# The starting addresses of TensorE's moving operands in SBUF, in a fused two-block kernel

## The chip, the cores and the metric

The kernel runs on one core of one Trainium2 chip. The metric is the device time of one execution in microseconds (us), as the median of several executions. Engines are named as in the profile: PE is TensorE's matmul side, PEld its weight loads, DVE VectorE, ACT ScalarE, POOL GpSimd, SP the queue that issues the DMAs.

## What is computed

Two transformer-like blocks run over one sequence of 256 tokens with 2048 features, all in float32. Cut to the matrix products that matter here:

```python
mod = silu(c) @ w_ada + b_ada                      # six modulation vectors
h = rmsnorm(x) * (1 + sc) + sh                     # 256 x 2048
q, k, v, g_ret, u, gate_r, gate_s = split(h @ w_in)
y_ret = (silu(g_ret) * norm(retention(q, k, v))) @ w_ret_out
y_s5  = glu(gelu(s5_ssm(u)) @ w_s5_glu)
x = x + gt * rmsnorm((sigmoid(gate_r)*y_ret + sigmoid(gate_s)*y_s5) @ w_out)
x = x + gt2 * rmsnorm((silu(a) * b) @ w_ffn_out)   # a, b = split(h2 @ w_ffn_in)
# second block: projections of h for attention, gated linear attention, convolution
mixed = g0 * (o_att @ w_br_attn) + g1 * (o_gla @ w_br_gla) + g2 * (y_conv @ w_br_conv)
x = x + mixed @ w_out_2
x = x + (silu(h4 @ w_gate) * (h4 @ w_up)) @ w_down
out = rmsnorm(x)
```

The weight matrices are large (703 MB are read), the 256 tokens few, so nearly all the time goes into products of a 128x128 piece of weights with 256 tokens.

## The kernel before

Features stand on the 128 partitions, the 256 tokens (T) in the free dimension. Every activation that is multiplied with large weights is kept as two float32r halves that together carry the float32 value: `h_split[P, 16, 512]` holds, for each of 16 tiles of features, 256 words of the high half and then 256 words of the low half. The same layout have `ffn1_split` and `ffn2_split` (the profile calls both ffn_split), `ret_split`, `merged_split`, `y_ssm_split`, `o_att_split`, `o_gla_split`, `y_conv_split` and `mixed_split`. These are the large moving operands.

Weights come through a ring of four slots. SP loads 1 MB into `ring_raw`, ACT writes the high half `ring_hi` (line 1017), DVE the low half `ring_lo` (line 1477), and PE uses them for one product. A product goes over 16 tiles of 128 features, and `products` (lines 632 to 639) is its inner step. It has two forms, which the text calls the pair and the triple:

- The pair, lines 638 and 639: the high weights times both halves of the moving operand (512 columns), then the low weights times the high half (256 columns), into two halves of one PSUM bank which DVE adds up later (line 1492). The stages from the first feed-forward on use it.
- The triple, lines 635, 636 and 637, three matmuls of 256 columns that add up in the same place. The stages `u`, `heads`, `ret`, `glu` and `out1` of the first block use it.

Both stream 768 moving columns per tile of 128 features. Each matmul has its own weight load of 128 columns. Everything else that PE does is small: sums of squares (lines 687 to 694), the retention, attention and gated-linear-attention products, the S5 steps (lines 705 and 715), the products of the value heads (line 734), and `gate_down` (lines 894 and 895), which multiplies `h_split` with only 16 columns of weights, `wa_hi` and `wa_lo`.

The order is written out by hand for each engine and tied by semaphores. Nothing in it depends on an address. SBUF is laid out by nested `with` blocks: `sb(stack, name, shape)` takes the next free place on the stack, rounded up to 32 bytes, and a block's places are free again when it closes. So a tensor's address is the sum of what was opened before it.

Of the kernel before, what the change touches and what calls it, by code (L numbers as in the profile page):

```python
# [29 lines left out]
P = 128  # L30
# [5 lines left out]
HEADS = 8  # L36
# [166 lines left out]
def program(nc, dram, out):  # L203
    stored, ph = schedule(), stages()
    with ExitStack() as ctx:
        def sb(stack, name, shape, dt=F32):
            return stack.enter_context(nc.sbuf_tensor(name, shape, dt))
# [26 lines left out]
        tile = [sb(ctx, f"tile{i}", [P, T]) for i in range(2)]  # L234
        eps = sb(ctx, "eps", [P, 4])
        root_of_one = sb(ctx, "root_of_one", [P, 1])

        with ExitStack() as shared:
            y2 = sb(shared, "y2", [P, KT, T])
# [6 lines left out]
        with ExitStack() as block1:  # L246
            c_act = sb(block1, "c_act", [P, D])
            with ExitStack() as mixer:
                log_g = sb(mixer, "log_g_sb", [P, HEADS])
                wv = [[], []]  # L250
                with ExitStack() as shared:
                    wv[0] = [sb(shared, f"wv_a{n}", [P, 4, 4, P]) for n in range(4)]
                with ExitStack() as shared:
                    v_heads = sb(shared, "v_heads", [P, HEADS, 4, T])
                with ExitStack() as shared:
                    ret = sb(shared, "ret_split", [P, HEADS, 2, 2 * T], F32R)
                with ExitStack() as shared:
                    first_gates = sb(shared, "first_gates", [P, 4, 2 * T])
                merged = sb(mixer, "merged_split", [P, KT, 2 * T], F32R)
                with ExitStack() as shared:  # L260
                    sb(shared, "y_ssm_first", [P, HALF // 2, 2 * T])
                    aside_y = sb(shared, "aside_y", [P, D])
                with ExitStack() as shared:
                    wv[1] += [sb(shared, f"wv_b{n}", [P, 4, 4, P]) for n in range(2)]
                y_ssm = sb(mixer, "y_ssm_split", [P, HALF, 2 * T], F32R)
                with ExitStack() as shared:
                    aside_z = sb(shared, "aside_z", [P, D])
                sb(mixer, "before_lag", [P, T])
                lag = sb(mixer, "lag_sb", [P, T])
                rope = sb(mixer, "rope_sb", [P, 2, T])  # L270
                with ExitStack() as shared:
                    aside_u = sb(shared, "aside_u", [P, D])
                with ExitStack() as shared:
                    wv[1].append(sb(shared, "wv_b2", [P, 4, 4, P]))
                u = sb(mixer, "u", [P, HALF, T])
                s5_a = sb(mixer, "s5_a_sb", [P, 3, S5_TILES])
                s5_d = sb(mixer, "s5_d_sb", [P, HALF])
                s5_turn = sb(mixer, "s5_turn", [P, 2, S5_TILES, RAMP])
                s5_r = sb(mixer, "s5_r", [P, S5_TILES])
                s5_f = sb(mixer, "s5_f", [P, S5_TILES, 2, 2])  # L280
                with ExitStack() as shared:
                    aside_s = sb(shared, "aside_s", [P, D])
                s5_b = [sb(mixer, f"s5_b_sb{i}", [P, 2, P]) for i in range(2)]
                s5_c = [sb(mixer, f"s5_c_sb{i}", [P, 2, P]) for i in range(2)]
                s5_prod = sb(mixer, "s5_prod", [P, 2, 2, 32])
                s5_x = [sb(mixer, f"s5_x{i}", [P, 2, T]) for i in range(2)]
                s5_y = sb(mixer, "s5_y", [P, T])
                s5_g = sb(mixer, "s5_g", [P, T])
                with ExitStack() as shared:
                    wv[1].append(sb(shared, "wv_b3", [P, 4, 4, P]))  # L290
                with ExitStack() as retention:
                    aside_r = sb(retention, "aside_r", [P, D])
                    qk_rot = sb(retention, "qk_rot", [P, 2, T])
                    g_act = sb(retention, "g_act", [P, 2, T])
                    scores = sb(retention, "scores", [P, 384])
                    o_t = sb(retention, "o_t", [P, 2, T])
                    gn_stats = sb(retention, "gn_stats", [P, 2, 6])
                    gn_mean = sb(retention, "gn_mean", [P, 2, 2])
                    gn_spare = sb(retention, "gn_spare", [P, 2])
                with ExitStack() as after:  # L300
                    m_ret = sb(after, "m_ret", [P, KT, T])
                    gate = sb(after, "gate", [P, T])
                    val_a = sb(after, "val_a", [P, T])
                    val_b = sb(after, "val_b", [P, T])
                with ExitStack() as before:
                    c_tanh_half = sb(before, "c_tanh_half", [P, D])
                    s5_t = sb(before, "s5_t", [P, 12, S5_TILES])
                    s5_step = sb(before, "s5_step", [P, RAMP])
                    s5_round = sb(before, "s5_round", [P, 2, S5_TILES, RAMP])
                with ExitStack() as after:  # L310
                    y1 = sb(after, "y1", [P, KT, T])
            with ExitStack() as ffn:
                f1 = sb(ffn, "ffn1_split", [P, FF, 2 * T], F32R)
                f1_a = [sb(ffn, f"ffn1_a{i}", [P, T]) for i in range(2)]
                f1_b = [sb(ffn, f"ffn1_b{i}", [P, T]) for i in range(2)]
                f1_t = [sb(ffn, f"ffn1_t{i}", [P, T]) for i in range(2)]


        with ExitStack() as block2:
            with ExitStack() as mixer:  # L320
# [27 lines left out]
                    a_end = sb(early, "a_end", [P, GLA_HEADS, T])  # L348
                t0 = sb(mixer, "merge0", [P, KT, T])
                conv_w = sb(mixer, "conv_w_sb", [P, HALF, 3])  # L350
                with ExitStack() as early:
                    gq = sb(early, "gq", [P, T])
                    gk = sb(early, "gk", [P, T])
                    gv_t = sb(early, "gv_t", [P, 2, T])
                    gr_t = sb(early, "gr_t", [P, 2, T])
                    gr_act = sb(early, "gr_act", [P, 2, T])
                    q_in = [sb(early, f"q_in{i}", [P, T]) for i in range(2)]
                    k_in = sb(early, "k_in", [P, T])
                    k_dec = sb(early, "k_dec", [P, T])
                    gv_n = sb(early, "gv_n", [P, 2, T])  # L360
                    k_dec_n = sb(early, "k_dec_n", [P, 3, P])
                    intra = sb(early, "intra", [P, 2, P])
                    state = [sb(early, f"state{i}", [P, T]) for i in range(3)]
                    go = sb(early, "go", [P, 2, T])
                    go_sq = sb(early, "go_sq", [P, 2, T])
                    go_std = sb(early, "go_std", [P, T])
                    go_rstd = sb(early, "go_rstd", [P, T])
                    att_q = [sb(early, f"att_q{i}", [P, T]) for i in range(2)]
                    att_k = [sb(early, f"att_k{i}", [P, T]) for i in range(2)]
                    att_v = [sb(early, f"att_v{i}", [P, T]) for i in range(2)]  # L370
# [2025 lines left out]
```

## Time and profile before

| | |
|---|---|
| median of three runs | 3384.47 us (3382.92 to 3384.51) |
| the profiled execution, whole | 3381.64 us |
| its span, first to last instruction | 3379.9 us |
| PE busy, share of the span | 98% |
| PEld / DVE / ACT / POOL busy | 87% / 69% / 43% / 13% |
| mean granted clock of PE | 0.992 of 2.4 GHz |
| DMA | 706 MB, mean 209 GB/s |

The trace gives each instruction's start and duration. A matmul's duration is longer than the step from its start to the next one's, because matmuls are pipelined. So what a matmul costs in a long stream is read from starts: the first start, a later one, and the number of matmuls between them. That step is what the text calls cadence.

### The profile page before, as it was taken

The page shows a single profiled execution, that of the slowest core. Times are in us where ns is not written, and L with a number is a line of the kernel's source. Part 1 is how long each engine was busy: PE and PEld are TensorE (multiplying, and loading weights), DVE is VectorE, ACT ScalarE, POOL GpSimd, SP SyncE. Part 2 cuts the span into 40 slices and gives each one's busy share as a digit, 9 for nine tenths or more (in the row PEclk, how much of TensorE's full clock was granted, in tenths as well). Part 3 has the DMA queues.
Part 4 walks back from the last instruction along what each step waited for, and adds up shares of the span by engine and source line. Part 5 has one row for each costly group of instructions (what it writes and reads, how often), then busy time and mean ns, then how long its engine had stood idle before and what let it go on. Part 6 is the DMA issues. An engine that isn't in the chain of part 4 may idle for free.

```text
span 3379.9 us, 51972 instructions
## 1 busy us (share of the span) xinstructions
PE 3307.3 (98%) x20368; PEld 2937.2 (87%) x20368; DVE 2324.5 (69%) x2503; ACT 1452.4 (43%) x1464; POOL 435.2 (13%) x309
## 2 busy tenths in 40 slices
PE   6999999999899999999899999999999999999998
PEld 3599999999788888888788888888888888888887
DVE  6789979877766666666666667566767766666554
ACT  2256664444443444433454443444344444344332
POOL 1047668500100000000000000000003000000000
PEclk9999999999999999999999999999999999999999
DMA  9885456678545555577534444555555555555554
GB/s 378 349 328 180 180 202 237 251 292 311 198 175 188 192 191 186 195 268 254 198 137 169 167 162 178 193 183 186 192 186 196 188 188 186 189 192 186 185 191 149
DMA packets 119746, 706.34 MB, mean 209 GB/s; under 512 B 13776, under 2 KB 28752, under 8 KB 41312
## 3 DMA queue, kind: packets, MB, share of 16 engines
q1 hardware_dynamic: 109280, 695.96, 56.2%
q10 hardware_dynamic: 10368, 9.02, 0.8%
q8 instruction: 68, 1.11, 0.1%
q14 instruction: 30, 0.25, 0.0%
HBM read 702.83 MB, written 2.10 MB: 209 GB/s over the span
## 4 chain that ended last, share of the span: by engine, by line
PE 90%; DVE 5%; ACT 1%; DMA 1%; SPq 1%; issue 1%; DVEq 0%; ACTq 0%
PE acc L638 45%; PE acc L639 24%; PE acc L635 6%; PE acc L636 6%; PE acc L637 6%; DVE ring_raw L1499 1%; DVE ring_lo L1477 1%; DMA ring_raw<-w_ada 1%; SPq L542 1%; PE p_y L705 1%; PE p_norm L687 1%; PE p_z L715 1%; ACT ring_hi L1017 0%; DMA ring_raw<-w_out 0%; DVE rstd L1524 0%
## 5 line engine op out<-in xcount | busy, mean ns | idle before, releaser
L638 PE MATMUL acc<-h_split,ring_hi 128*128 128x512 f32 x4736 | 1655.9, 392 | 9.5 <-DVE h_split L1539 4.5
L1477 DVE TENSOR_TENSOR ring_lo<-ring_raw,ring_hi 128x2048 fp32r<-128x2048 f32 (+2 forms) x560 | 1265.1, 2260 | 550.2 <-ACT ring_hi L1017 549.1
L639 PE MATMUL acc<-h_split,ring_lo 128*128 128x256 f32 x4736 | 1337.6, 282 | 0.0
L1017 ACT ACTIVATE ring_hi<-ring_raw 128x2048 fp32r<-128x2048 f32 (+2 forms) x560 | 1040.0, 1862 | 458.6 <-DMA ring_raw<-w_down 150.4
L638 PEld LDWEIGHTS acc<-h_split,ring_hi 128*128 128x128 f32 x4736 | 891.9, 188 | 197.6 <-issue 10.0
L639 PEld LDWEIGHTS acc<-h_split,ring_lo 128*128 128x128 f32 x4736 | 897.9, 190 | 0.4
L638 PE MATMUL acc<-ffn_split,ring_hi 128*128 128x512 f32 x1408 | 488.2, 390 | 0.0
L2146 POOL TENSOR_TENSOR sq_sum<-sq_sum,tile 128x256 f32<-128x256 f32 x60 | 79.6, 1326 | 2561.6 <-ACT tile L1043 2561.6
L639 PE MATMUL acc<-ffn_split,ring_lo 128*128 128x256 f32 x1408 | 397.1, 282 | 0.0
L635 PE MATMUL acc<-h_split,ring_hi 128*128 128x256 f32 x1152 | 329.2, 286 | 0.3 <-ACT val_a L1030 0.2
L637 PE MATMUL acc<-h_split,ring_lo 128*128 128x256 f32 x1152 | 321.6, 279 | 0.0
L636 PE MATMUL acc<-h_split,ring_hi 128*128 128x256 f32 x1152 | 321.6, 279 | 0.0
L638 PEld LDWEIGHTS acc<-ffn_split,ring_hi 128*128 128x128 f32 x1408 | 264.4, 188 | 55.4
L639 PEld LDWEIGHTS acc<-ffn_split,ring_lo 128*128 128x128 f32 x1408 | 266.1, 189 | 0.0
L635 PEld LDWEIGHTS acc<-h_split,ring_hi 128*128 128x128 f32 x1152 | 216.6, 188 | 1.8 <-issue 0.6
L636 PEld LDWEIGHTS acc<-h_split,ring_hi 128*128 128x128 f32 x1152 | 216.6, 188 | 1.1 <-issue 0.2
L637 PEld LDWEIGHTS acc<-h_split,ring_lo 128*128 128x128 f32 x1152 | 216.6, 188 | 0.0
L1310 ACT ACTIVATE ffn_split<-ffn_a 128x256 f32 (+1 forms) x88 | 36.8, 418 | 361.5 <-DVE ffn_a L1903 361.5
L1492 DVE TENSOR_REDUCE ffn_b<-acc 128x256 f32<-128x512 f32 x88 | 60.8, 691 | 143.2 <-PE acc L639 143.2
L1043 ACT ACTIVATE tile<-x_res 128x256 f32 (+1 forms) x80 | 33.1, 417 | 152.1 <-DVE x_res L2127 85.2
L1308 ACT ACTIVATE ffn_t<-ffn_a 128x256 f32<-128x256 f32 x88 | 36.7, 417 | 129.3 <-DVE ffn_a L1899 119.2
L2204 POOL TENSOR_TENSOR s_x<-s_w,s_tab 128x512 f32<-128x512 f32 x32 | 86.6, 2707 | 29.9 <-DVE s_w L1688 29.8
(381 smaller groups left out, 3936.5 us busy)
## 6 DMA issues: line engine op xcount, KB each, us to landing
ring_raw<-w_ff SPq DMA_DIRECT2D x88, 1024.0 KB, 4.8
ring_raw<-w_down SPq DMA_DIRECT2D x64, 1024.0 KB, 4.8
ring_raw<-w_ffb SPq DMA_DIRECT2D x56, 1024.0 KB, 4.8
ring_raw<-w_mix SPq DMA_DIRECT2D x48, 1024.0 KB, 4.8
ring_raw<-w_ada SPq DMA_DIRECT2D x32, 1024.0 KB, 11.9
ring_raw<-w_heads SPq DMA_DIRECT2D x32, 1024.0 KB, 4.8
ring_raw<-w_ret SPq DMA_DIRECT2D x32, 1024.0 KB, 5.2
ring_raw<-w_glu SPq DMA_DIRECT2D x32, 1024.0 KB, 4.9
```

The costliest lines, as they stand in the source:

```text
L635: mm(dst[:, 0:T], hi[s][:, t, :], moving[:, k, 0:T], start=start, stop=False)
L636: mm(dst[:, 0:T], hi[s][:, t, :], moving[:, k, T:], start=False, stop=False)
L637: return mm(dst[:, 0:T], lo[s][:, t, :], moving[:, k, 0:T], start=False, stop=stop)
L638: mm(dst[:], hi[s][:, t, :], moving[:, k, :], start=start, stop=False, skip_group_check=True)
L639: return mm(dst[:, T:], lo[s][:, t, :], moving[:, k, 0:T], start=False, stop=stop, skip_group_check=True)
L1017: run(hi[s][:, 0:n, :], raw[s][:, 0:n, :], COPY).then_inc(hi_done, 1)
L1308: run(t[i % 2][:], a[i % 2][:], ACT.Tanh, scale=0.5).then_inc(f_tanh, 1)
L1310: run(dst[:, 4 * g + (first + i), 0:T], a[i % 2][:], COPY, scale=0.5).then_inc(f_hi, 1)
L1477: tt(lo[s][:, 0:n, :], raw[s][:, 0:n, :], hi[s][:, 0:n, :], SUB).then_inc(lo_done, 1)
L1492: v.tensor_reduce(dst, acc[o % 2][:].rearrange("p (c t) -> p t c", c=2), AX_X, ADD).then_inc(sum_done, 1)
L2146: tt(sq_sum[:], sq_sum[:], tile[b][:], ALU.add).then_inc(sq_used, 1)
L2204: tt(xs[:], w[:], sin, ALU.mult)
```

## The change

Three lines are added and one is moved. `log_g` (8 words, 32 bytes) is taken before `h_split` and not in the mixer of block 1, and two unused tensors of 32 bytes are put in. No instruction is added, taken away or moved: on every engine the instructions stand in the same order with the same waits, and only addresses differ.

```diff
@@ -234,6 +234,7 @@
         eps = sb(ctx, "eps", [P, 4])
         root_of_one = sb(ctx, "root_of_one", [P, 1])
+        log_g = sb(ctx, "log_g_sb", [P, HEADS])
...
@@ -246,7 +247,6 @@
             with ExitStack() as mixer:
-                log_g = sb(mixer, "log_g_sb", [P, HEADS])
                 wv = [[], []]
...
@@ -275,6 +275,7 @@
                 s5_d = sb(mixer, "s5_d_sb", [P, HALF])
+                sb(mixer, "s5_space", [P, 8])
                 s5_turn = sb(mixer, "s5_turn", [P, 2, S5_TILES, RAMP])
...
@@ -348,6 +349,7 @@
                 conv_w = sb(mixer, "conv_w_sb", [P, HALF, 3])
+                sb(mixer, "conv_space", [P, 8])
                 with ExitStack() as early:
```

The addresses of the built programs, as the remainder by 128. Each operand's tiles are 2048 bytes apart and its low half begins 1024 bytes behind the high one, so every matmul on it starts at the same remainder.

| tensor | form | before | after |
|---|---|---|---|
| `h_split` | pairs and triples | 32 | 64 |
| `ffn1_split`, `ffn2_split` | pairs | 32 | 64 |
| `o_att_split`, `o_gla_split`, `y_conv_split` | pairs | 32 | 64 |
| `mixed_split` | pairs | 0 | 64 |
| `ret_split`, `merged_split`, `y_ssm_split` | triples | 64 | 64 |
| `wv_a`, `u` (float32, moving) | small products | 64 | 64 |
| `s5_x` (float32, moving) | S5 steps | 96 | 0 |
| `ring_raw`, `ring_hi`, `ring_lo` (weights) | all | 0 | 0 |
| `wa_hi`, `wa_lo` (weights of `gate_down`) | 16 columns | 32 | 64 |
| `x_res`, `tile`, `rstd` | | 0, 96, 96 | the same |

The smaller tensors that lie above these on the stack shift by 32 or 64 bytes with them.

## Rows read from the trace of the kernel before

**Rows 1.** The page: busy time; the chain that ended last, by engine and line.
```profile
PE 3307.3 (98%) x20368; PEld 2937.2 (87%) x20368; DVE 2324.5 (69%) x2503; ACT 1452.4 (43%) x1464; POOL 435.2 (13%) x309
PE 90%; DVE 5%; ACT 1%; DMA 1%; SPq 1%; issue 1%; DVEq 0%; ACTq 0%
PE acc L638 45%; PE acc L639 24%; PE acc L635 6%; PE acc L636 6%; PE acc L637 6%; DVE ring_raw L1499 1%; DVE ring_lo L1477 1%; DMA ring_raw<-w_ada 1%; SPq L542 1%; PE p_y L705 1%; PE p_norm L687 1%; PE p_z L715 1%; ACT ring_hi L1017 0%; DMA
```

**Rows 2.** Groups of PE by shape: count | busy us, mean ns | idle us.
```profile
L638 PE MATMUL acc<-h_split,ring_hi 128*128 128x512 f32 x4736 | 1655.9, 392 | 9.5 <-DVE h_split L1539 4.5 <-DVE h_split L1537 4.4 <-DVE ffn_a L1492 0.4
...
L638 PE MATMUL acc<-ffn_split,ring_hi 128*128 128x512 f32 x1408 | 488.2, 390 | 0.0
...
L636 PE MATMUL acc<-h_split,ring_hi 128*128 128x256 f32 x1152 | 321.6, 279 | 0.0
...
L636 PE MATMUL acc<-ret_split,ring_hi 128*128 128x256 f32 x256 | 71.5, 279 | 0.0
...
L636 PE MATMUL acc<-merged_split,ring_hi 128*128 128x256 f32 x256 | 70.7, 276 | 0.0
```

**Rows 3.** Timeline of PE, pairs on h_split: start us, us, engine, line.
```profile
999.84 0.39 PE L638 MATMUL acc<-h_split,ring_hi 128*128 128x512 f32 x1
...
1032.77 0.39 PE L638 MATMUL acc<-h_split,ring_hi 128*128 128x512 f32 x1
```

**Rows 4.** Timeline of PE, pairs on mixed_split, the first product's 16.
```profile
2542.53 0.40 PE L638 MATMUL acc<-mixed_split,ring_hi 128*128 128x512 f32 x1
...
2548.14 0.39 PE L638 MATMUL acc<-mixed_split,ring_hi 128*128 128x512 f32 x1
```

**Rows 5.** Timeline of PE, triples in the glu stage: h_split, y_ssm_split, h_split again.
```profile
703.80 0.28 PE L635 MATMUL acc<-h_split,ring_hi 128*128 128x256 f32 x1
...
709.41 0.28 PE L635 MATMUL acc<-y_ssm_split,ring_hi 128*128 128x256 f32 x1
...
714.85 0.28 PE L635 MATMUL acc<-h_split,ring_hi 128*128 128x256 f32 x1
```

**Rows 6.** Timeline of PE, one product of triples on ret_split, and what follows it.
```profile
464.76 0.28 PE L635 MATMUL acc<-ret_split,ring_hi 128*128 128x256 f32 x1
...
470.41 0.38 PE L705 MATMUL p_y<-s_x,s_c_sb 128*128 128x256 f32 x1
```

**Rows 7.** Timeline of PE, the slowest product of triples on h_split.
```profile
692.60 0.28 PE L635 MATMUL acc<-h_split,ring_hi 128*128 128x256 f32 x1
...
698.35 0.28 PE L635 MATMUL acc<-y_ssm_split,ring_hi 128*128 128x256 f32 x1
```

**Rows 8.** Timeline of PE, gate_down: pairs on h_split with 16 columns of weights.
```profile
1699.47 0.39 PE L894 MATMUL p_score<-h_split,wa_hi 128*16 128x512 f32 x1
...
1704.69 0.39 PE L894 MATMUL p_score<-h_split,wa_hi 128*16 128x512 f32 x1
```

**Rows 9.** Timeline of PE: float32 products of 512 columns; then pairs at half clock.
```profile
79.66 1.02 PE L734 MATMUL p_o<-wv_b,normed 128*128 128x512 f32 x2
...
81.37 1.02 PE L734 MATMUL p_z<-wv_b,normed 128*128 128x512 f32 x2
...
1731.24 0.41 PE L639 MATMUL acc<-h_split,ring_lo 128*128 128x256 f32 x1
...
1733.80 0.41 PE L639 MATMUL acc<-h_split,ring_lo 128*128 128x256 f32 x1
```

**Rows 10.** Waits of PE; stretches, busy of PE PEld DVE ACT POOL, PEclk, DMA.
```profile
PE acc L638 <- DVE h_split L1539: 4.5, 1, 4.5
...
1731.30:1733.70 2.40, 2.40 (x9) 2.11 (x8) 1.92 (x2) 2.40 (x7) 0.00 (x0) 0.50 0.00 0
...
2300.00:2500.00 200.00, 200.00 (x1156) 177.31 (x1155) 139.70 (x154) 79.69 (x72) 0.00 (x0) 1.00 0.52 189
```

**Rows 11.** Two groups of ACT on the page, of the same form.
```profile
L1310 ACT ACTIVATE ffn_split<-ffn_a 128x256 f32 (+1 forms) x88 | 36.8, 418 | 361.5 <-DVE ffn_a L1903 361.5
...
L1043 ACT ACTIVATE tile<-x_res 128x256 f32 (+1 forms) x80 | 33.1, 417 | 152.1 <-DVE x_res L2127 85.2
```

## The prediction

> **What bounds the kernel now.** First the page's busy times and the chain of waits: PE is busy for 98% of the span and carries 90% of the chain that ended last, 87% of it in the five lines of `products` [rows 1]. So the question is what one of these matmuls costs, and next how many there are of each kind: the groups by shape [rows 2] give 4736 pairs on h_split and 1408 on ffn_split. o_att, o_gla and y_conv have 16 products of 8 pairs each, 384, which makes 6528 pairs at remainder 32. mixed_split has 16 products of 16 pairs, 256, at remainder 0. h_split has also 1152 triples at 32 [rows 2], which is 72 products of 48 matmuls.
>
> The durations in the groups don't give the cost, since matmuls overlap. The timeline does. From 999.84 to 1032.77 lie 95 pairs on h_split: 32.93 us / 95 = 346.6 ns each [rows 3]. The product on mixed_split, at remainder 0, has 16 pairs in 5.61 us, 350.6 ns each [rows 4]. Both ran at full clock, with the same ring of weights, 768 columns, no wait inside. The address is the one difference I can name, so a pair feels it, by 4 ns between 0 and 32. What a pair costs at 64 no row shows: all pairs of this kernel stand at 0 or 32.
>
> The triples do show 64. Side by side in the glu stage, 48 matmuls on h_split (remainder 32) take 5.61 us, 116.9 ns each, and the 48 behind them on y_ssm_split (64) take 5.44 us, 113.3 ns [rows 5]. All 16 products on merged_split and the last 11 of 16 on y_ssm_split look like that; the mean duration goes with it, 276 ns in the middle matmul on merged_split [rows 2]. But 64 has a second, slower cadence: a product on ret_split takes 5.65 us, 117.7 ns each [rows 6]. 15 of 16 products on ret_split, with a mean of 279 [rows 2], and the first 5 on y_ssm_split have it. merged_split has the same address as ret_split, so the address alone doesn't decide which cadence a product falls into. Remainder 32 has a slow cadence too, 5.75 us or 119.8 ns [rows 7], but in one product of 72, and in no stretch of pairs.
>
> Is the loss in the weight loads? `gate_down` loads 16 columns of weights in place of 128 and still takes 5.22 us for 15 pairs, 348.0 ns [rows 8]. So shorter loads don't help, and what is lost is on the side of the moving operand. Is it a fixed price of each matmul? Float32 products of 512 columns pass twice: from the first of two on p_o to the first of two on p_z, with two on p_norm between, four start in 1.71 us, 427.5 ns each for 1024 column steps [rows 9], hardly above 1024 / 2.4. At half clock four pairs take 2.56 us, 640 ns each [rows 9], which is 768 / 1.2 exactly; the granted clock there is 0.50 [rows 10]. The overhead is there only when float32r columns are asked for at 2.4 per ns: a pair takes 346.6 where 768 / 2.4 is 320.0. That fits a reader of SBUF that can't quite keep up and for which the start within some unit matters. The Trainium skill ("TensorE: Matmul & The Clock Gate", Back-to-back issue gap) gives N / 2.4 + 2.5 ns for a warm matmul, whatever the address. By that a pair would take 325.0 before and after and the change would do nothing. The measured 346.6 and 350.6 decide against it.
>
> **The change part by part.** No instruction moves, so every term is a count times a change of cadence, on the engine that sets the end.
>
> Pairs from 32 to 64, 6528 of them. The bounds: nothing below 320.0 (a gain of 26.6 ns) and, above, three matmuls at 117.7, 353.1 (a loss of 6.5). Between them two readings of the good cadence. A triple at 64 takes 3 x 113.3 = 340.0 for the same 768 columns. Or a pair keeps its relation to a triple, which at 32 is 346.6 / 350.7: then it takes 340.0 x 346.6 / 350.7 = 336.0. I take 340.0, since it is the row itself, and keep 336.0 for the range: 6528 x 6.6 = 43.1 us saved.
>
> Pairs on mixed_split from 0 to 64, 256: 256 x (350.6 - 340.0) = 2.7 us saved.
>
> Triples on h_split from 32 to 64, 72 products. The 61 that stand before 690 us in the trace share their stages with ret_split and the early y_ssm_split, whose 64 was slow in 20 of 21. I let them follow: 61 x 48 x (117.7 - 116.8) = 2.6 us lost. The 11 later ones gain: 11 x (5.61 - 5.44) = 1.9 us saved. Together 0.7 us lost. If all were at 113.3, they would save 61 x 48 x 3.5 + 1.9 = 12.1 us, and ret_split and y_ssm_split another 20 x 48 x 4.4 = 4.2 us.
>
> What stays at nothing: ret_split, merged_split and y_ssm_split keep their remainder. s5_x goes from 96 to 0, but its float32 products pass at half rate like those of [rows 9], and the longest of them are a few hundred matmuls. In the few pairs at half clock the address can't show, since their 640 ns hold no overhead [rows 9]. The shifted tensors of ACT and DVE: ACT takes 418 ns to write ffn_split at 32 and 417 to write tile at 96 [rows 11], so I give them no cost. Both engines have slack anyway: in a typical stretch of 200 us DVE is busy 139.7 and ACT 79.7, at 189 GB/s [rows 10].
>
> Is a shorter product covered by the others? A product of 16 pairs would go from 5.55 to 5.44 us. DVE needs 139.7 / 200 x 5.55 = 3.9 of it. PE waits for no low half of the ring in the steady stages: the largest wait of a product is a stage's opening, 4.5 us [rows 10]. DMA would go from 189 to 193 GB/s. So the gain arrives whole. Those waits stay.
>
> The sum: -43.1 - 2.7 + 0.7 = -45.1 us against the profiled execution's 3381.6, which is 3336.5. The median lies 2.8 above that execution, so 3339.
>
> **The rivals.**
>
> Deeper: pairs at 336.0 and all triples at 113.3: 6528 x 10.6 + 256 x 14.6 + 16.3 = 89.2 us saved, 3295. For it speaks that a pair is one matmul less than a triple and was 4.1 ns cheaper at 32. Halfway to it lies 3317.
>
> The slow cadence (the other side): pairs at 64 lock into the one that ret_split shows. Scaled as above, 353.1 x 346.6 / 350.7 = 349.0, a loss of 2.4 ns a pair. 6528 x 2.4 = 15.7 us lost, 0.4 won on mixed_split, 72 x 48 x 0.9 = 3.1 lost on h_split, and 5.9 (28 x 48 x 4.4) if the fast products at 64 fell too: 24.3 us, 3409. It decides above 347.6 ns for a pair: from there the kernel is slower by over 0.2%. For it: 20 of 48 products at 64 are slow, and I know no cause. Against: they all lie in the first 690 us, in and just behind the S5 stages. From there on all 27 products at 64 are fast, and the stages of pairs all lie later. And pairs at 32 hold one cadence through every wait.
>
> Nothing happens: 32 and 64 are alike for a pair, and the gap between the triples comes from something else in the stage. Then only the triples move, from 0.7 lost to 16.3 saved: 3385, or 3367. The mechanism would be a unit of 16 or 32 bytes, of which 0, 32 and 64 are all multiples. The Trainium skill ("SBUF — State Buffer", in the part on the DMA port swizzle) states lines of 16 bytes, and by it alone the change leaves the time at 3384. Against it: mixed_split at 0 and h_split at 32 differ in the same form and the same ring [rows 3, 4].
>
> That the change doesn't do what it says I leave out: the addresses of the built program show all of the large operands at 64.
>
> **How the numbers follow.** Chances: the forecast 0.42, the deeper case 0.15, pairs unchanged with triples gaining 0.08, nothing 0.12, the slow cadence 0.20, something slower still 0.03. A measurement of this kernel can tell about 0.2% from no change, 6.8 us. Faster: 0.42 + 0.15 + 0.08 = 0.65. Same: 0.12, and 0.01 of the slow case. Slower: 0.22. The range goes from 3300, which cuts off the deep end, to 3412, which takes in the slow case. The likeliest case alone has 3315 to 3350.
>
> **What would show it.** In the trace after, the timeline of a stretch like [rows 3]: 95 pairs should take 32.3 us, not 32.9; the product on mixed_split 5.44 us, not 5.61; h_split in glu 5.44, not 5.61. A window like that from 2300 us should hold about 1177 matmuls in 200 us, not 1156 [rows 10]. If the pairs show 349 or more, the step that failed is the carrying over of a triple's cadence to a pair. If pairs are faster and the span isn't, PE has new waits on the low halves of the ring, from DVE.

## The result, and the profile after

The changed kernel takes 3431.26 us (median of four, 3429.51 to 3434.0) against 3384.07 for the kernel before on the same occasion: a ratio of 1.0141, 95% interval 1.0123 to 1.0158. It is slower by 47 us, where 45 us less were forecast. The span of the profiled execution grew from 3379.9 to 3432.2, by 52.3 us. That is 5 us more than the medians differ: the profile before is of one of that kernel's quicker executions (3381.64 us), the profile after of the slowest of four (3434.0). Every cadence below is read from one execution of its kernel.

The page after, the rows that answer to [rows 1]; line numbers are two higher than before.

```profile
PE 3358.9 (98%) x20368; PEld 2949.1 (86%) x20368; DVE 2327.5 (68%) x2503; ACT 1452.1 (42%) x1464; POOL 433.0 (13%) x309
PE 90%; DVE 5%; DMA 2%; ACT 1%; SPq 1%; issue 1%; DVEq 0%; ACTq 0%
```

PE's busy time grew by 51.6 us, that of its loads by 11.9, and no other engine's by more than 3.0. The bound is the same, and it is the matmuls that cost more. The wait of PE that [rows 10] shows and one stretch, in the changed kernel:

```profile
PE acc L640 <- DVE h_split L1541: 4.5, 1, 4.5
...
2300.00:2500.00 200.00, 200.00 (x1134) 174.15 (x1133) 136.59 (x152) 79.36 (x71) 0.00 (x0) 1.00 0.50 184
```

1134 matmuls in 200 us, where 1156 stood before and 1177 were forecast. In this stretch DVE and ACT are less busy and the clock is full. PE's waits for other engines add up to 60.4 us before and 61.1 after, so they explain under 1 us. Single ones did move: a wait of a small product on p_norm, before and then after, grew by 3.8 us, and two others shrank by 3.2 together.

```profile
PE p_norm L765 <- DVE o_t L1730: 0.4, 1, 0.4
```

```profile
PE p_norm L767 <- DVE o_t L1732: 4.2, 1, 4.2
```

The timelines of PE in the changed kernel, for [rows 3, 4, 5]: pairs on h_split, pairs on mixed_split, triples on h_split in the glu stage.

```profile
999.75 0.39 PE L640 MATMUL acc<-h_split,ring_hi 128*128 128x512 f32 x1
...
1032.96 0.40 PE L640 MATMUL acc<-h_split,ring_hi 128*128 128x512 f32 x1
...
2589.79 0.40 PE L640 MATMUL acc<-mixed_split,ring_hi 128*128 128x512 f32 x1
...
2623.71 0.40 PE L640 MATMUL acc<-mixed_split,ring_hi 128*128 128x512 f32 x1
...
709.12 0.28 PE L637 MATMUL acc<-h_split,ring_hi 128*128 128x256 f32 x1
...
714.77 0.28 PE L637 MATMUL acc<-y_ssm_split,ring_hi 128*128 128x256 f32 x1
```

94 pairs on h_split in 33.21 us are 353.3 ns each (346.6 before). 96 pairs on mixed_split in 33.92 us are 353.3 (350.6). 48 matmuls in 5.65 us are 117.7 (116.9). Both traces hold the same 20368 matmuls in the same order, so the steps can be compared one by one. Over the whole trace the steps of the 6528 pairs grew by 42.4 us, about 6.5 ns a pair, and those of the 256 on mixed_split by 0.6 us. Alone in a stream a pair grew by 6.7 ns; between small matmuls it grew less (h_split at 352.4 ns there in the changed kernel).

Another part came from operands whose address didn't change. Triples on merged_split (their third matmuls), before and then after:

```profile
839.98 0.28 PE L637 MATMUL acc<-merged_split,ring_lo 128*128 128x256 f32 x1
...
845.76 0.28 PE L637 MATMUL acc<-merged_split,ring_lo 128*128 128x256 f32 x1
```

```profile
839.75 0.28 PE L639 MATMUL acc<-merged_split,ring_lo 128*128 128x256 f32 x1
...
845.75 0.28 PE L639 MATMUL acc<-merged_split,ring_lo 128*128 128x256 f32 x1
```

Both fences hold 17 triples: 5.78 us, 340.0 ns each, and 6.00 us, 353 ns. All of merged_split and y_ssm_split is at 353.3 ns now, so 27 products of 16 triples lost 13.3 ns each: 5.7 us. The triples on h_split took 2.4 us more. Together that is 51.1 of the 52.3 us; the rest lies in the small products and in the waits. Neither merged_split nor the ring moved by a byte between these two kernels. So the 5.7 us need not be the doing of the change. The spans of the two profiles differ by 5 us more than the medians, which is about as much, and there is no second trace of either kernel to show whether these triples have the same cadence in each execution.

### The profile page after: what moved, and what is told of

Same layout as the page of the kernel before. It is cut to its first block, busy times and chain, and to the rows that moved or that the text cites. A ratio compares the mean times of both kernels' runs of the same rounds, so it can differ in the third digit from the quotient of the medians.

```text
span 3432.2 us, 51972 instructions
## 1 busy us (share of the span) xinstructions
PE 3358.9 (98%) x20368; PEld 2949.1 (86%) x20368; DVE 2327.5 (68%) x2503; ACT 1452.1 (42%) x1464; POOL 433.0 (13%) x309
## 4 chain that ended last, share of the span: by engine, by line
PE 90%; DVE 5%; DMA 2%; ACT 1%; SPq 1%; issue 1%; DVEq 0%; ACTq 0%
PE acc L640 46%; PE acc L641 24%; PE acc L637 5%; PE acc L638 5%; PE acc L639 5%; DVE ring_raw L1501 1%; DVE ring_lo L1479 1%; DMA ring_raw<-w_ada 1%; SPq L544 1%; PE p_y L707 1%; PE p_z L717 1%; PE p_norm L689 1%; ACT ring_hi L1019 0%; DMA ring_raw<-w_u 0%; DVE rstd L1526 0%
## 5 line engine op out<-in xcount | busy, mean ns | idle before, releaser
L640 PE MATMUL acc<-h_split,ring_hi 128*128 128x512 f32 x4736 | 1688.3, 398 | 9.4 <-DVE h_split L1541 4.5
L640 PE MATMUL acc<-ffn_split,ring_hi 128*128 128x512 f32 x1408 | 497.6, 396 | 0.0
L640 PE MATMUL acc<-mixed_split,ring_hi 128*128 128x512 f32 x256 | 90.5, 397 | 0.0
```

Source lines behind the costliest of these rows:

```text
L640: mm(dst[:], hi[s][:, t, :], moving[:, k, :], start=start, stop=False, skip_group_check=True)
```

## The experiments

The question is what the address of the moving operand is counted from. Two facts of the timeline give the candidates: in long streams of these two kernels pairs have one cadence at one address, and the load of the next weights starts with the matmul (2 to 4 ns behind its start in the changed kernel). The changed kernel at 1000 us:

```profile
1000.10 0.40 PE L640 MATMUL acc<-h_split,ring_hi 128*128 128x512 f32 x1
1000.10 0.19 PEld L641 LDWEIGHTS acc<-h_split,ring_lo 128*128 128x128 f32 x1
1000.33 0.28 PE L641 MATMUL acc<-h_split,ring_lo 128*128 128x256 f32 x1
1000.34 0.19 PEld L640 LDWEIGHTS acc<-h_split,ring_hi 128*128 128x128 f32 x1
```

So two streams are read from SBUF at once, the moving operand and the next weights. Theory A: the moving operand's own remainder decides. Theory B: the distance between the two streams decides. Theory C: the way a stage is entered decides. All kernels below are the changed kernel with other spacers, unless said otherwise. In the kernel before and in the change every ring tensor has the remainder 128 by 256. "Distance" is the moving operand's address less the weights', from the second group on modulo 256.

**All operands at 32, 96, 0, and the weights at 32.** One more spacer behind `log_g`, of 96, 32 and 64 bytes. The fourth has 32 bytes ahead of the ring and 96 behind `log_g`.

```diff
+        sb(ctx, "ring_space", [P, 8])          # r32_m64 only
         raw, hi, lo = [], [], []
...
         log_g = sb(ctx, "log_g_sb", [P, HEADS])
+        sb(ctx, "moving_space", [P, 24])       # m32, r32_m64; 8 in m96, 16 in m0
```

> All large moving operands at remainder 32, the ring of weights at 0 as before. Theory A (the moving operand's own remainder by 128 sets the cadence) and theory B (the distance between moving operand and weights sets it) agree here: pairs 346.7 ns, those on mixed_split too (before 351.0), triples about 350, time within 3 us of 3384. Theory C (the cadence is a matter of how a stage is entered, not of addresses): pairs keep any of 346.7 or 353.3, so a stage or two may differ.

Measured: ratio to before 1.0015 (1.0005 to 1.0024). All pairs at 346.7 ns, those on mixed_split too. The triples are slower than before, at 352 to 354 ns.

> All large moving operands at remainder 96, weights at 0. Theory B, if distances of 32 to either side count alike: pairs 346.7 ns as at 32, about 3385 us. Theory A says nothing on 96 ahead of the run; if the cadence goes with the number of 64-byte units touched, 96 is like 32 (346.7), if it grows with the remainder it is above 353.3, over 3431 us.

Measured: 1.0109 (1.0092 to 1.0126). Pairs 350.0 ns, but 353.0 on mixed_split; triples 360.0, near the slow cadence of [rows 7], in every product. Neither guess of the expectation, 346.7 or above 353.3, was right.

> All large moving operands at remainder 0, weights at 0. Both A and B carry over what mixed_split showed before: pairs 351.0 ns, so 6528 x 4.3 = 28 us over before, about 3412 us. Theory C: pairs at 346.7 or 353.3.

Measured: 1.0105 (1.0088 to 1.0122). Pairs 351.1 ns as expected, 353.3 on mixed_split, triples 356. The time is 3419.83 us, 8 more than expected; the slower triples were not in the estimate.

> Moving operands at remainder 64 as in the change, but the ring of weights at 32 (and x_res, ident, ones and the other tensors behind it 32 further on). The distance between the two is 32, as before the change. Theory A: pairs 353.3 ns, about 3431 us. Theory B: pairs 346.7 ns, about 3384 us.

Measured: 1.0009 (0.9999 to 1.0018). Pairs 346.7 ns, with the moving operands at remainder 64. That is against theory A and for B. The same stretch in m96, m0 and r32_m64, with 1145, 1141 and 1156 matmuls:

```profile
1000.00:1200.00 200.00, 200.00 (x1145) 174.26 (x1144) 125.75 (x126) 81.86 (x71) 0.00 (x0) 1.00 0.52 187
```

```profile
1000.00:1200.00 200.00, 200.00 (x1141) 175.27 (x1141) 127.13 (x125) 80.41 (x71) 0.00 (x0) 1.00 0.52 185
```

```profile
1000.00:1200.00 200.00, 200.00 (x1156) 176.03 (x1155) 127.51 (x127) 82.45 (x72) 0.00 (x0) 1.00 0.53 190
```

mixed_split was the odd one out: it had the same remainder by 128 as the others and another cadence. By 256 its address differs from theirs by 128. Ordered by distance modulo 256, the pairs of all these runs fall into one table.

| distance from both kinds of weights | ns a pair | seen on |
|---|---|---|
| 0 | 353.3 | mixed_split in m0 |
| 32 | 346.7 | kernel before; mixed_split in m32 and r32_m64 |
| 64 | 353.3 | change |
| 96 | 350.0 | m96 |
| 128 | 351.1 | m0; mixed_split in the kernel before |
| 160 | 346.7 | m32, r32_m64 |
| 192 | 353.2 | mixed_split in the change |
| 224 | 353.0 | mixed_split in m96 |

**Low and high weights apart, first try.** Spacers within each slot of the ring, so that the high weights lie 32 bytes off the low ones by 128.

```diff
             lo.append(sb(ctx, f"ring_lo{s}", [P, KT, P], F32R))
+            sb(ctx, f"hi_space{s}", [P, 8])    # hi32_lo0; 24 in hi0_lo32
             hi.append(sb(ctx, f"ring_hi{s}", [P, KT, P], F32R))
+            sb(ctx, f"lo_space{s}", [P, 24])   # hi32_lo0; 8 in hi0_lo32
```

hi0_lo32 has besides 32 bytes ahead of the ring and 96 behind `log_g`.

> The changed kernel, moving operands at 64, low weights at 0, high weights at 32. So the distance from the weights to the moving operand is 64 for the low and 32 for the high weights. PE starts the load of the next weights 2 to 3 ns after a matmul's start. Theory B1 (what counts is the distance to the weights that are loaded during a matmul): the 512-column step runs beside a load of low weights at distance 64 and stays near 233.6 ns, the 256-column step runs beside a load of high weights at distance 32 and falls to about 118; pair about 352, time about 3423 us. Theory B2 (what counts are a matmul's own weights): 512-column step about 229, 256-column step 119.7, pair about 348.5, 3400 us.

Measured: 1.0076 (1.0059 to 1.0093), pairs 350.0 ns in both feed-forward blocks and in the long streams on h_split beside them, but from 347.3 (h_split) to 353.4 (o_gla) in the stages between.

> The mirror of the kernel with high weights at 32: low weights at 32, high weights at 0, moving operands at 64. B1: 512-column step about 229, 256-column step 119.7, pair about 348.5, 3400 us. B2: pair about 352, 3423 us. If the two mixtures come out alike, the load and the stream couple over the whole pair and neither theory splits it rightly.

Measured: 1.0056 (1.004 to 1.0073), pairs 349.8 ns, from 348.8 to 350.8 by operand. In the feed-forward blocks the two mixtures came out alike. But by 256 the slots lie 128 apart in turn here, so each kernel mixes two distances. They decide nothing between B1 and B2.

**Distances of 16 and 48.** The ring's tensors begin 16 or 48 bytes into their space, by a view. By 256 the high weights then lie 128 bytes from the low ones.

```diff
...
-            lo.append(sb(ctx, f"ring_lo{s}", [P, KT, P], F32R))
+            lo.append(sb(ctx, f"ring_lo{s}", [P, KT * P + 4], F32R)[:, 4:].rearrange("p (k c) -> p k c", k=KT))
+            sb(ctx, f"lo_space{s}", [P, 24])
...
```

> Moving operands at 64, all ring weights at 16: distance 48. If the cadence runs smoothly between the distances measured (32: 346.7, 64: 353.3), the pair is near 350.0 and the time near 3408 us. If only the unit of 32 bytes counts, which a distance falls into, it is one of the two, 346.7 or 353.3.

Measured: 1.0035 (1.0024 to 1.0046). Distance 48 from the low and 176 from the high weights, and two cadences at the same addresses: 351.1 ns in the first feed-forward block, 346.7 in the second. The changeover lies between 1742 and 2059 us, in the stages where each product is followed by small matmuls. mixed_split, at 176 from the low and 48 from the high weights, has 344.5, the fastest pair seen. The run had 1141 matmuls in the first stretch and 1156 in the second:

```profile
1000.00:1200.00 200.00, 200.00 (x1141) 174.76 (x1140) 126.05 (x126) 81.15 (x72) 0.00 (x0) 1.00 0.52 187
...
2300.00:2500.00 200.00, 200.00 (x1156) 175.55 (x1155) 140.06 (x155) 80.17 (x73) 0.00 (x0) 1.00 0.52 189
```

> Moving operands at 64, all ring weights at 48: distance 16. Between 0 (351.1) and 32 (346.7): 348.9 if smooth, about 3400 us; else one of the two.

Measured: 1.0124 (1.0104 to 1.0145). Distances 16 and 144, pairs 353.3 ns; mixed_split, at 144 and 16, has 348.9. In these two kernels each operand has two distances at once, so they are no points of the table. But no mixture of table values gives 344.5, which is below all of them: steps of 16 bytes matter.

**Low and high weights apart, all slots alike.** As in the first try, but the two spacers of a slot add up to 256 bytes (56 and 8 words in lo32_hi64, 8 and 56 in lo64_hi32); lo32_hi64 has 224 bytes more behind `log_g`.

> Distances now counted modulo 256, since the earlier runs differ for mixed_split, which lies 128 further on than the other operands. Low weights at distance 32, high weights at 64, the same for all four slots (in the kernels with one kind of weights shifted by 32 the slots lay 128 apart in turn). Theory B1 (the weights loaded beside a matmul count): 512-column step as at 32, 228.3 ns, 256-column step as at 64, 119.7; pair 348, time about 3395 us. Theory B2 (its own weights count): 233.6 + 118.3 = 352, 3422 us.

Measured: 1.0055 (1.0035 to 1.0075). Pairs 348.9 ns in all stages but on mixed_split, which stands at 160 and 192 and has 353.3. In the 348.9 lie a 512-column step of 231.4 and a 256-column step of 117.5. B1 wanted 228.3 and 119.7, B2 233.6 and 118.3.

> The mirror: low weights at distance 64, high weights at 32. B1: 352 ns, about 3422 us. B2: 348 ns, about 3395 us. If neither holds, the two steps of a pair can't be told apart this way.

Measured: 1.0072 (1.0046 to 1.0098). Pairs at 346.7 ns in both feed-forward blocks and mostly at 353.3 between them (348.0 on mixed_split). Both B1 and B2 fall: a pair's two steps don't split into a share for each kind of weights. At the same addresses h_split has 346.7 up to 1700 us, 353.3 from 2080 us on, and 346.7 again behind the stage of mixed_split. So it depends on what went before, as in r16_m64; what exactly, no run shows. From 1000 us and from 2300 us, on h_split in both, 1156 and 1133 matmuls:

```profile
1000.00:1200.00 200.00, 200.00 (x1156) 175.84 (x1155) 127.82 (x127) 82.81 (x73) 0.00 (x0) 1.00 0.53 189
...
2300.00:2500.00 200.00, 200.00 (x1133) 173.48 (x1133) 136.37 (x151) 79.36 (x71) 0.00 (x0) 1.00 0.51 184
```

**The fastest distances for all.** The ring of r16_m64, with `moving_space` of 128 bytes and `conv_space` grown by 128, so that every moving operand is at 176 and 48.

> All moving operands at distance 176 from the low and 48 from the high weights, which only mixed_split had in the kernel with weights at 16, at 344.5 ns a pair. If the distances modulo 256 decide, all pairs take 344.5: 6784 x 2.2 = 15 us less than before the change, triples a few us either way, 3370 to 3376 us. If something else made mixed_split fast there, pairs are at 346.7 or above and the time 3384 us or more.

Measured: 3374.23 us, ratio to the kernel before 0.9967 (0.9955 to 0.998). It is the only kernel here that is faster than the kernel before. Its pairs on h_split, 96 of them in 33.06 us, 344.4 ns each:

```profile
999.80 0.39 PE L643 MATMUL acc<-h_split,ring_hi 128*128 128x512 f32 x1
...
1032.86 0.39 PE L643 MATMUL acc<-h_split,ring_hi 128*128 128x512 f32 x1
```

The other operands have it too, mixed_split included. All triples are at 353.3, which gives back part of the 15 us.

**Each operand at a distance of its own.** Spacers and views before each operand; the ring as before.

> Each operand at a distance of its own from both kinds of weights, modulo 256: h 48, ffn1 176, ffn2 112, o_att 80, o_gla 208, y_conv 240, mixed 16. If the distance alone decides, each operand has one cadence throughout its stages, between 340 and 354 ns a pair, and changes within a pair or two where the operand changes. If the history decides, operands behind one another keep the same cadence. No time is expected beyond 3380 to 3430 us.

Measured: 3414.03 us in a single execution. Pairs: h 350.6 on average (351.1 in long streams, 347.5 to 350 between small matmuls), ffn1 350.0, ffn2 353.3, o_att 351.8, o_gla 353.5, y_conv 349.9, mixed 346.8. Operands right behind one another keep differing, which history alone doesn't explain. Distance 16 is as good as 32 and 160 within 0.1 ns; none here is as good as the pair 176 and 48.

**The deciding pair.** 32 bytes ahead of everything, in the kernel before and in the change.

```diff
+        sb(ctx, "all_space", [P, 8])
         raw, hi, lo = [], [], []
```

> The kernel before with 32 bytes ahead of everything. h_split, ffn_split, o_att, o_gla and y_conv stand at the very addresses that they have in the change (remainder 64), and all distances to the weights are those of the kernel before. If the distance decides: pairs 346.7 ns, mixed_split 351.0, merged_split 340.0 or 353.3, 3380 to 3392 us. If the moving operand's own address decides: 353.3 ns, 3431 us.

Measured: 0.9998 (0.9989 to 1.0008), pairs 346.7, mixed_split 351.1. h_split and the other four stand at the same addresses as in the change. From the first row to the last lie 95 pairs, 32.93 us, as in [rows 3]:

```profile
999.91 0.39 PE L639 MATMUL acc<-h_split,ring_hi 128*128 128x512 f32 x1
...
1032.84 0.39 PE L639 MATMUL acc<-h_split,ring_hi 128*128 128x512 f32 x1
```

> The changed kernel with 32 bytes ahead of everything: moving operands at remainder 96, weights at 32, distance 64 as in the change. If the distance decides: pairs 353.3 ns, about 3431 us. If the moving operand's own remainder decides: 350.0 ns as in the kernel with all moving operands at 96, 3421 us.

Measured: 1.0131 (1.0114 to 1.0148), pairs 353.3. 94 pairs in 33.21 us, to the digit as in the change:

```profile
999.61 0.39 PE L641 MATMUL acc<-h_split,ring_hi 128*128 128x512 f32 x1
...
1032.82 0.40 PE L641 MATMUL acc<-h_split,ring_hi 128*128 128x512 f32 x1
```

So theory A is out. At one address of the moving operand, to the byte, a pair takes 346.7 or 353.3 ns as the weights, and all else that lies ahead of it, stand 32 bytes further on or not.

One rival is left: the other traffic on SBUF. DVE, ACT and the DMAs write the ring, so their addresses moved with the weights. The traces settle it. In the streams on h_split and ffn_split from 900 to 1650 us and from 2700 to 3300 us, take only the pairs during which neither DVE, ACT or POOL nor any DMA engine of the core shows work: 142 pairs of the kernel before have 346.7 ns, 162 of the changed kernel 353.3, as all others have. So the difference doesn't need that traffic; what is left are PE's own reads.

`gate_down` says whose weights count. Its weights `wa_hi` and `wa_lo` move together with h_split, and their tiles are 64 bytes apart, so that its pairs go through four distances, the same ones before and after. The ring stands at another distance after the change, yet the 15 steps of [rows 8] take 5.24 us where they took 5.22:

```profile
1723.89 0.40 PE L896 MATMUL p_score<-h_split,wa_hi 128*16 128x512 f32 x1
...
1729.13 0.39 PE L896 MATMUL p_score<-h_split,wa_hi 128*16 128x512 f32 x1
```

In every kernel in which these distances are kept they take 347.2 to 349.3 ns a pair, while pairs on the ring go from 344.4 to 353.3; in map16, which changes them, they take 345.1. So the distance to the weights that are loaded for the stream itself fits, and the distance to the ring does not. With 16 columns in place of 128 the loads are shorter here, which may dampen the effect.

before_32on shows another thing as well. The triples on merged_split and y_ssm_split have the same distance as in the kernel before (64), yet all run at 353 ns and not at 340. Its 17 triples on merged_split take 6.01 us:

```profile
839.87 0.28 PE L638 MATMUL acc<-merged_split,ring_lo 128*128 128x256 f32 x1
...
845.88 0.28 PE L638 MATMUL acc<-merged_split,ring_lo 128*128 128x256 f32 x1
```

With equal distances that leaves theory C, or chance, for this part: at some distances two cadences are stable. That what went before a product settles which one it takes is argued, not shown. In the trace of the kernel before, y_ssm_split itself changes from 353 to 340 after its fifth product. And before_32on, all slow here, has the same median as the kernel before within 1 us, though 27 products at 340 ns would make 5.7 us: the fast cadence may belong to the execution that was profiled.

## Why the prediction was wrong

**What held.** PE's matmuls are the bound, no cover came into play, the waits add up to 0.7 us more, and the steps of pairs and triples account for 51.1 of 52.3 us. The reading that a pair feels the address held. So did the reading that there is a second, slower cadence. Its bound from above, three matmuls at 117.7, 353.1 ns, is where the pairs landed.

**What failed first** is the term for the pairs from 32 to 64, 43.1 us saved. It is the step that the prediction had named for the case that pairs show 349 or more: the carrying over of a triple's cadence to a pair. The term took 340.0 ns a pair from triples on merged_split and y_ssm_split. The pairs measured 353.3, and the term came out as 42.4 us lost; mixed_split, put at 2.7 us saved, lost 0.6. The cadence of 340.0 exists for triples at distance 64, and it was in the changed kernel too: in the `u` stage, 16 triples take 5.44 us.

```profile
170.75 0.28 PE L637 MATMUL acc<-h_split,ring_hi 128*128 128x256 f32 x1
...
176.19 0.28 PE L637 MATMUL acc<-h_split,ring_hi 128*128 128x256 f32 x1
```

But the slow one is as stable, and the pairs at 64 took it in the two kernels that had them there, with the products of h_split that small matmuls follow at 351 or 352. No pair at distance 64 from both kinds of weights showed the fast one in a long stream. I had both cadences in the rows, 28 products of 48 against 20, and read the fast one as the rule for later stages. The position in time was no reason: before_32on has the slow one in the same late stages.

**The rival's price.** The slow cadence was forecast at 24.3 us, since I scaled 353.1 down to 349.0 by the relation of pair to triple at 32. That relation doesn't hold at 64: pair and triple both take 353.3. The loss of 2.4 ns a pair was 6.7 in long streams, and 15.7 us were 42.4. The rival's other terms were near: the fast products on merged_split and y_ssm_split, counted as 5.9 us, lost 5.7 between the two profiles, and the triples on h_split, 3.1 us, lost 2.4. So the rival had the mechanism, a slow cadence, and mis-sized it for pairs.

**The step beneath it** was the frame. "The address is the one difference I can name" compared mixed_split at remainder 0 with h_split at 32, both by 128. The weights' addresses stood in the same table, all at 0, and so the distance and the remainder were the same number and could not be told apart. By 256, which the table didn't show, h_split was at distance 32 and mixed_split at 128. Remainder 32 was not a middle value on the way to a better 64: distance 32 is, of the eight steps of 32 bytes, one of the two best.

**The dismissal of the weight loads.** From the short loads of `gate_down` [rows 8] I concluded that the loss is on the moving operand's side alone. What the row shows is that short loads don't remove it; and its weights stand at four distances in turn, single steps take 340 to 352 ns, so its mean is no match for a stream at one distance. The runs show that where the loads read from changes a pair by 6.6 ns. The Trainium skill ("TensorE: Matmul & The Clock Gate", Step-by-step: what each phase is for) says that the two read ports are independent and that loading the next weights doesn't steal bandwidth from the running matmul. before_32on against the change shows 346.7 and 353.3 ns for the same matmuls on the same moving addresses, and the difference is there with all other engines and the DMAs quiet. So in this kernel the two are not independent.

**What stays open.** That the pair's cadence follows the distance to the weights is shown; that the two streams collide in SBUF is argued from it. No run took the loads away. Why 32 and 160 are good, how low and high weights share in it, and what switches between two stable cadences isn't known. The repeats of one kernel spread by some 10 us (before: 3380.8 to 3390.1), those of r16_m64, r48_m64 and lo64_hi32 by 12.3 to 12.5. A cadence locked in differently from one execution to the next could do that, but it wasn't tested.

## What to carry to other kernels

In a long stream of float32r matmuls the cost of one is read from starts in the timeline, over a whole product, and an overhead above columns / 2.4 is worth looking at: here it was 24.4 to 33.3 ns on 320. Here it depended on where the moving operand lies relative to the weights (a count modulo 256 bytes fits all runs), so a spacer of a few bytes cost 1.4% or brought 0.3%, and any edit of the layout above the ring can do so by accident. A cadence seen in one form of matmul is not to be carried to another at the same address, least of all where the rows show two of them.

## What the runs showed of the hardware

- Cadence of a pair (768 float32r columns, 320.0 ns at 2.4 GHz) by distance: 344.4 ns (low 176, high 48) to 353.3 (64 or 0; 353.5 at 208). No position tried was free of overhead. It is the same while DVE, ACT, POOL and DMA are quiet.
- The triple of 256-column matmuls: 340.0 or 353.3 ns at distance 64, 352 to 356 at 160, 356 at 128, 360.0 at 96. Its best and worst are further apart than the pair's.
- At some distances two cadences are stable for hundreds of microseconds at unchanged addresses: 351.1 and 346.7 (low 48, high 176), 346.7 and 353.3 (low 64, high 32), 340.0 and 353.3 (triples at 64).
- Float32 products, which pass at half rate (256 columns in about 216 ns), didn't follow any of this: those on `u` start 215.5 to 216.0 ns apart on average in every kernel.
